# A ninth weight buffer, buffers in order of release, and the short expert's first gate and up moved into the long expert's first step

## What is computed

```python
def moe_swiglu(h, w_router, w_gate, w_up, w_down):
    logits = (t @ w_router)                       # 256 x 8
    top_vals, top_idx = lax.top_k(logits, TOP_K)  # 2 of 8
    top_w = jax.nn.softmax(top_vals, axis=-1)
    for e in range(N_EXPERTS):
        out = out + swiglu(t, w_gate[e], w_up[e], w_down[e]) * gates[:, e:e + 1]
return rms_norm(x, final_norm_g)
```

## Time and profile before

| | us |
|---|---|
| Median of 3 runs | 1364.99 (1363.95 to 1365.55) |
| The profiled execution | 1365.68 |
| Its span, first to last instruction | 1363.8 |
| PE busy | 1325.5 (97%) |
| VectorE busy | 787.8 (58%) |
| ScalarE busy | 658.2 (48%) |
| The queue of SP's transfers | 440.82 MB, 79.7% of 16 engines' span |
| Mean granted TensorE clock | 0.996 |

### The profile page before, as it was taken

How to read it: one execution, slowest core, us unless ns; L and a number is a source line. 1 busy time by engine, 2 the same in 40 slices (tenths; PEclk the granted TensorE clock), 3 DMA queues, 4 the chain that set the end, 5 groups by cost and what they waited for, 6 DMA issues and landing times.

```text
span 1363.8 us, 16923 instructions
## 1 busy us (share of the span) xinstructions
PE 1325.5 (97%) x6365; PEld 945.1 (69%) x6365; DVE 787.8 (58%) x912; ACT 658.2 (48%) x823; POOL 41.2 (3%) x45
## 2 busy tenths in 40 slices
PE   9999999999999999999999999999999999999996
PEld 8888788888888778765666656666555566665562
DVE  6555445555569668856466455565444565554463
ACT  5444344444454756544455454454444455544451
POOL 1000001000000010200000000000000000000000
PEclk9999999999999999999999999999999999999999
DMA  9745456555455518999999999999999999999995
GB/s 382 300 155 185 158 181 229 193 192 189 147 192 188 214 71 332 380 420 425 410 429 427 428 427 426 412 426 427 429 428 426 412 427 426 430 426 428 427 426 213
DMA packets 40448, 451.63 MB, mean 331 GB/s; under 512 B 4873, under 2 KB 5001, under 8 KB 8368
## 3 DMA queue, kind: packets, MB, share of 16 engines
q1 hardware_dynamic: 37408, 440.82, 79.7%
q0 software_dynamic: 2816, 9.63, 1.8%
q10 hardware_dynamic: 144, 0.09, 0.0%
HBM read 445.52 MB, written 6.55 MB: 331 GB/s over the span
## 4 chain that ended last, share of the span: by engine, by line
PE 78%; DMA 17%; DVE 2%; ACT 1%; issue 1%; POOL 0%; SPq 0%; DVEq 0%; ACTq 0%
PE psum L1968 19%; PE psum L1970 18%; PE psum L1969 18%; PE psum L2356 15%; DMA raw<-in_moe_w_gu 6%; DMA raw_more<-in_moe_w_gu 4%; DMA raw_first<-in_moe_w_gu 2%; DMA work<-in_moe_w_gu 2%; DMA raw<-in_moe_w_down 2%; PE psum L2014 1%; PE psum L2015 1%; PE psum L2016 1%; PE psum L2024 1%; DVE w_lo L1386 1%; ACT w_hi L1023 1%; PE psum L2394 1%
## 5 line engine op out<-in xcount | busy, mean ns | idle before, releaser
L1386 DVE TENSOR_TENSOR w_lo<-raw,w_hi 128x1024 fp32r<-128x1024 f32 (+1 forms) x150 | 265.7, 1782 | 224.2 <-ACT w_hi L1023 223.5
L1023 ACT CAST w_hi<-raw 128x1024 fp32r<-128x1024 f32 (+1 forms) x150 | 223.1, 1498 | 225.5 <-PE psum L1970 156.2
L1970 PE MATMUL psum<-w_hi,actA_lo 128*128 128x512 f32 (+1 forms) x752 | 291.2, 387 | 0.0
L1968 PE MATMUL psum<-w_hi,actA_hi 128*128 128x512 f32 (+1 forms) x644 | 257.1, 399 | 21.8 <-DVE w_lo L1386 20.6
L1969 PE MATMUL psum<-w_lo,actA_hi 128*128 128x512 f32 (+1 forms) x644 | 248.7, 386 | 0.0
L1968 PEld LDWEIGHTS psum<-w_hi,actA_hi 128*128 128x128 f32 x644 | 121.8, 189 | 66.3 <-DVE w_lo L1386 32.2
L1970 PEld LDWEIGHTS psum<-w_hi,actA_lo 128*128 128x128 f32 x752 | 141.9, 189 | 30.1
L1969 PEld LDWEIGHTS psum<-w_lo,actA_hi 128*128 128x128 f32 x644 | 122.2, 190 | 22.0
L2356 PE MATMUL psum<-raw,const 128*64 128x512 f32 x584 | 129.4, 595 | 0.1
L1968 PE MATMUL psum<-w_hi,actB_hi 128*128 128x512 f32 x292 | 114.8, 393 | 0.0
L1969 PE MATMUL psum<-w_lo,actB_hi 128*128 128x512 f32 x292 | 114.0, 390 | 0.0
(11 more groups left out here) (280 smaller groups left out, 1987.2 us busy)
## 6 DMA issues: line engine op xcount, KB each, us to landing
raw<-in_moe_w_gu SPq DMA_DIRECT2D x46, 2048.0 KB, 25.0
raw_more<-in_moe_w_gu SPq DMA_DIRECT2D x35, 2048.0 KB, 25.0
raw<-in_moe_w_down SPq DMA_DIRECT2D x23, 2048.0 KB, 26.4
raw_first<-in_moe_w_gu SPq DMA_DIRECT2D x17, 2048.0 KB, 25.6
raw_more<-in_moe_w_down SPq DMA_DIRECT2D x16, 2048.0 KB, 26.2
work<-in_moe_w_gu SPq DMA_DIRECT2D x14, 2048.0 KB, 27.0
raw<-in_ret_w_in SPq DMA_DIRECT2D x22, 1024.0 KB, 9.3
work<-in_moe_w_down SPq DMA_DIRECT2D x9, 2048.0 KB, 27.1
```

The lines of the kernel that those rows point to most:

```text
L1023: nc.scalar.copy(hi_of(u)[:, 0:size], raw_of(w, u)[:, 0:size]).then_inc(sem["hi_ready"], 1)
L1386: nc.vector.tensor_tensor(lo_of(u)[:, 0:size], raw_of(w, u)[:, 0:size], as_f32(hi_of(u)[:, 0:size]), ALU.subtract).then_inc(sem["lo_ready" ...
L1968: nc.tensor.matmul(dst, l_hi[:, k, cols], r_hi[:, kk, rcols], start=first, stop=False)
L1970: return nc.tensor.matmul(dst, l_lo[:, k, cols], r_hi[:, kk, rcols], start=False, stop=last)
```

## The change

- The buffers get a ninth one, number 8, over `work[0:4096]`, for blocks 13, 19 and 25 only. Block 13 waits until both gathers and the writing of the rows to DRAM are done.
- The buffers of blocks 5 to 48 come from a written table in place of the cycle. Blocks 5 and 6 go into buffers 7 and 0, and block 9 is issued behind them.
- The loop and the last pair use eight buffers for their first blocks (56 of 84 in a turn of the loop, 8 in the last pair) and seven for the rest.
- The final gain goes into buffer 4, and POOL loads it at the end, behind the read of y.
- TensorE's first steps: 4 parts of step 0; `short_gather`; a fifth part; the short gate and up; the last 3 parts; 4 parts of step 1; the turning of step 0; the other 4 parts; 4 down parts; the turning of step 1; the slot sums. Step 1's gate and up use other PSUM banks.
- ScalarE copies the short rows and the short gate and up in that place. VectorE ranks the places between the two halves of the long rows' residue and picks the short rows ahead of the third part's residue; its gate arithmetic, up to `rest_of_current(0)`, moves from behind the 20th part's residue to behind the ninth part's.

```diff
@@ work_order @@
         open_hidden("first", 0, G0, U0)
-        parts(8, ("first", "long_gate", 0), ("first", "long_up", 0))
-        open_hidden("first", 1, G1, U1)
+        parts(4)
+        o.open(("short_gather",), T1, ("short_rows", 1))
+        o.group(("short_gather",))
+        parts(1)
+        short_hidden("first", 0)
+        parts(3, ("first", "long_gate", 0), ("first", "long_up", 0))
+        open_hidden("first", 1, U1, T1)
         parts(4)
         long_turn("first", 0)
-        o.open(("short_gather",), T1, ("short_rows", 1))
-        o.group(("short_gather",))
...
         long_turn("first", 1)
-        short_hidden("first", 0)
@@ the tables @@
-        def ring_first(v):
-
-            return v if v < 5 else (0, 1, 5, 6, 7, 2, 3, 4)[(v - 5) % FIRST_RAW]
+        ring_first = [0, 1, 2, 3, 4, 7, 0, 5, 6, 1, 7, 0, 2, 8, 3, 4, 5, 6, 1, 8, 7, 0, 2, 3, 4, 8, 5, 6, 1, 7, 0, 2, 3, 4, 5,
+                      6, 2, 1, 7, 0, 3, 4, 1, 5, 6, 2, 7, 0, 3]
+        ring_more, ring_last = ring_first[-MORE_RAW:], ring_first[-EXPERT_RAW:]
+        ring_loop = ring_more * MORE_TURNS + ring_last * ((2 * ITEM_BLOCKS - MORE_TURNS * MORE_RAW) // EXPERT_RAW)
+        ring_end = ring_more + ring_last * (ITEM_BLOCKS // EXPERT_RAW)
...
-                + [work[:, 6400:6400 + 2 * UNIT]] + [more[:, :] for more in raw_more[0:2]])
-        final_gain = raw_more[1][:, 0:D]
+                + [work[:, 6400:6400 + 2 * UNIT]] + [more[:, :] for more in raw_more[0:2]]
+                + [work[:, 0:2 * UNIT]])
+        final_gain = twos[ring_more[0]][:, 0:D]
@@ SP @@
+                elif ring_first[v] == FIRST_RAW - 1:
+                    sp.wait_ge(sem["pe_done"], w.pe("short_gather"))
+                    sp.wait_ge(sem["rows_out"], 16 * TILES)
...
+            def user_before(v):
+
+                before = [u for u in range(v) if ring_first[u] == ring_first[v]]
+                if before:
+                    first_used(before[-1])
+                else:
+                    first_free(v)
...
-            first_free(FIRST_BLOCKS + 2)
-            load(FIRST_BLOCKS + 2, "down", None, 1, 0, False)
+            first_free(5)
             sp.wait_ge(sem["ranked"], 1)
             short_first = sp.value_load(expert_ids[0:1, 3 * EXPERT_PAIRS:3 * EXPERT_PAIRS + 1], min_val=0, max_val=N_EXPERTS - 1)
             for v in range(5, FIRST_BLOCKS):
-                long_split(n_dense + 4 * (v - 5) + 3)
+                if v > 5:
+                    user_before(v)
                 load(v, FIRST[v][0], short_first, *FIRST[v][2:], False)
+            user_before(FIRST_BLOCKS + 2)
+            load(FIRST_BLOCKS + 2, "down", None, 1, 0, False)
             load_pair(0)
@@ POOL @@
             move_rows(0)
-            pool.wait_ge(sem["pe_done"], w.pe("pair", "short_gu", STEPS - 1, 1))
-            load_gain(1)
...
+            pool.wait_ge(sem["pe_done"], w.pe("last", "short_gu", 2, 0))
             pool.wait_ge(sem["two_in"][w.ring(v)], w.block_in(v))
             pool.sem_inc(sem["back_asked"], 1)
             pool.dma_start(y_back.rearrange("p t k d -> p t (k d)"),
                            y_dram[P:, :].rearrange("(t p k) d -> p t (k d)", t=TILES, k=2)).then_inc(sem["y_in"], 16)
+            load_gain(1)
@@ ScalarE @@
+            hi_through(n_dense + 8)
+            short_rows(("short_gather",))
+            hi_through(n_dense + 9)
+            short_gu_out("first", 0)
             hi_through(n_dense + 11)
             long_silu("first", 0)
             hi_through(n_dense + 16)
             turned_hi("first", 0)
-            short_rows(("short_gather",))
             hi_through(n_dense + 19)
             long_silu("first", 1)
             hi_through(n_dense + 20)
             turned_hi("first", 1)
             hi_through(n_dense + 24)
-            short_gu_out("first", 0)
@@ TensorE @@
-                for half in range(2):
-                    pe.wait_ge(sem["long_lo"], half + 1)
-                    long_hidden("first", 0, units, range(4 * half, 4 * half + 4))
+                pe.wait_ge(sem["long_lo"], 1)
+                long_hidden("first", 0, units, range(4))
+                short_gather(("short_gather",))
+                pe.wait_ge(sem["long_lo"], 2)
+                long_hidden("first", 0, units, range(4, 5))
+                pe.wait_ge(sem["short_rows"], 1)
+                short_hidden("first", 0, 5)
+                long_hidden("first", 0, units, range(5, KC))
                 long_hidden("first", 1, units, range(4))
                 turn_hidden("first", 0)
-                short_gather(("short_gather",))
                 long_hidden("first", 1, units, range(4, KC))
                 long_down("first", 0, units, range(4))
                 turn_hidden("first", 1)
-                pe.wait_ge(sem["short_rows"], 1)
-                short_hidden("first", 0, 5)
                 slot_sums(("slots",), 0)
```

More of the change, by code:

```diff
@@ L617, in block_in, with place @@
             def block_in(self, v):
-                r = self.ring(v)
+                ring, i = self.place(v)
+                r = ring[i]
+                n = 16 * (ring[:i + 1].count(r) + (0 if ring is ring_first else first_loads[r]))
+                return n if self.turn is None else self.turn * (16 * loop_loads[r]) + n
+            def place(self, v):
                 if self.base == 0 and v < LOOP_BLOCK:
-                    return 16 * sum(self.ring(before) == r for before in range(v + 1))
-                n = first_loads[r] + 1 + (v - FIRST_BLOCKS) // EXPERT_RAW + (self.base - 1) * (ITEM_BLOCKS // EXPERT_RAW)
-                return 16 * n if self.turn is None else self.turn * (32 * ITEM_BLOCKS // EXPERT_RAW) + 16 * n
+                    return ring_first, v
+                if self.last:
+                    return ring_end, v - FIRST_BLOCKS
+                return ring_loop, v - FIRST_BLOCKS + (self.base - 1) * ITEM_BLOCKS
             def ring(self, v):
-                if self.base == 0 and v < LOOP_BLOCK:
-                    return ring_first(v)
-                return (2, 3, 4, 0, 1, 5, 6)[(v - FIRST_BLOCKS) % EXPERT_RAW]
+                ring, i = self.place(v)
+                return ring[i]
             def part_done(self, u):
@@ L896, in _ @@
                 load_pair(2)
-            w.turn, w.base, j = turns, 1, 0
+            w.turn, w.base, w.last, j = turns, 1, True, 0
             now, seen = experts_of(0), set()
@@ L989, in _ @@
                 move_rows(2)
-            w.turn, w.base = turns, 1
+            w.turn, w.base, w.last = turns, 1, True
             pool.wait_ge(sem["y_done"], w.at("y_done", 16 * 4))
             v = FIRST_BLOCKS + END_DOWN + 4
+            pool.wait_ge(sem["pe_done"], w.pe("last", "short_gu", 2, 0))
             pool.wait_ge(sem["two_in"][w.ring(v)], w.block_in(v))
@@ L1354, in _ @@
                 pair(2)
-            w.turn, w.base, w.units, split[0] = turns, 1, order.last_units, first_loop_unit + EXPERT_SPLIT
+            w.turn, w.base, w.units, w.last, split[0] = turns, 1, order.last_units, True, first_loop_unit + EXPERT_SPLIT
             for n in range(2, STEPS):
@@ L1800, in _ @@
             lo_through(n_dense + 2)
-            for g in range(2):
-                long_rows_rest(("gather",), g, 0)
+            long_rows_rest(("gather",), 0, 0)
+            in_rank_order(place_ranked, place)
+            long_rows_rest(("gather",), 1, 0)
             dve.sem_inc(sem["short_out"], 1)
-            lo_through(n_dense + 10)
-            in_rank_order(place_ranked, place)
+            lo_through(n_dense + 3)
             for t in range(TILES):
@@ L2513, in _ @@
                 pair(2)
-            w.turn, w.base, count[:] = turns, 1, loop_start
+            w.turn, w.base, w.last, count[:] = turns, 1, True, loop_start
             units = done + order.last_units
```

48 lines of the change are left out of this document (30 added, 18 removed).

## The result

| | before | after |
|---|---|---|
| Median of 22 runs each, us | 1364.82 (1362.93 to 1367.02) | 1366.93 (1363.3 to 1369.96) |
| Ratio, 95% interval | | 1.0015 (1.0009 to 1.0021) |
| The profiled execution, us | 1365.68 | 1366.78 |
| Its span, us | 1363.8 | 1365.0 |
| Mean granted TensorE clock | 0.996 | 0.993 |

The kernel became about 2 us slower (by the interval 1.2 to 2.9). The forecast was 1363.3 us with a range to 1366.2; the median lies outside it. By the 0.2% of the prediction (2.7 us) this is "no change", but 22 runs on each side tell even 0.15% apart from nothing. The two profiled executions differ by 1.1 us, and that is what can be followed in the trace.

The account below looks back on a forecast made before the run. The prediction took the start of the unbroken weight stream plus the bytes behind it as the bound. Anchor -0.45 and final gain -1.2 sum to -1.65 us, against the median of 1364.99 giving 1363.3 us, range 1360.5 to 1366.2.

Parts of the forecast that it names:

- What bounds the kernel: Whole kernel: the end is the time at which the weight stream starts to be unbroken, plus the bytes behind it.
- The new anchor: Start of the unbroken stream: block 19, issued behind block 13's last residue, lands at 597.95 + D; gain 2.35 - D, 0.45 us.
- D = +1.9: Ahead of the loop: its first step starts 1.9 us later than before, first product at 567.9.
- the cover is gone: Ahead of the loop: 7 us of short products no longer hide the last turning and copy before the first cast.
- upper bound of 2.3: Ahead of the loop: the most that the first step's delay D was allowed to be, 2.3 us.
- finds room: Kernel's end: the final gain's 512 KB, moved behind y, lands at 1349.7 in free DMA time; 1.2 us saved.
- slower rival: Kernel's end: the final gain lands at 1360.4, after its first use; +4.6 us, in all 1367.9 us; chance 0.06.
- near 545: Before the loop: the rows are written to DRAM near 545, so block 13's wait for them costs nothing.
- Blocks 5 and 6 early: Before the loop: blocks 5 and 6 land at 532.4 and 537.3, in time for the short products; effect nothing.
- the loop's eight buffers: In the loop: an eighth buffer gains nothing, since TensorE waits for bytes and the DMA engines are never idle.
- the rival of the late register reading: Before the loop: SP reads the expert's number late, block 5 is issued at 529.1; D 4.4, time 1365.8 us; chance 0.10.
- The rule of the Trainium skill that was weighed: In the loop: the added buffer would remove TensorE's 20.6 us of waits, giving 1344.4 us; as a rival, chance 0.03.

Follow-up runs that it names:

- late_block: casts_first with block 19's issue made to wait for the split of block 14's first part, 8.3 us later: 1369.48 us, ratio 1.0039 to the kernel before.
- filler: The changed kernel with eleven useless TensorE products in the pause ahead of the loop: 1364.91 us, ratio 0.9998 to the kernel before.
- rows_swap: casts_first with blocks 13 and 14 trading buffers (19, 23, 25 following), so block 13 skips the wait for the rows' writing: 1362.98 us, ratio 0.9984.
- release_order: casts_first with the buffer table rewritten so block 13 doesn't wait for the rows nor block 19 for block 13: 1361.36 us (0.9972), repeated 1361.07 us (0.9977).
- loop_only: The kernel before with only eight buffers for part of the loop and last pair, and the final gain behind y: 1364.92 us, ratio 0.9999.
- first_only: The changed kernel with seven buffers in the loop and the final gain loaded behind the first pair, as before: 1366.87 us, ratio 1.0013.
- casts_first: The changed kernel with the loop's first four casts and residues moved ahead of the copy of the last turned rows: 1362.52 us, ratio 0.9981.
- gain_early: casts_first with the final gain loaded ahead of the last blocks instead of behind the read of y: 1363.93 us, ratio 0.9991.

## Why the prediction was wrong

- **What bounds the kernel** (right). The start of the unbroken stream plus the bytes: a hole of 8.3 us in the stream, with no engine's work touched, costs 7.8 us at the end (late_block).
- **The new anchor is block 19 behind block 13's last residue** (right). Issue 0.16 us behind the residue, queue empty ahead of it.
- **D = +1.9, "the cover is gone"** (mechanism right, term mis-sized). The first product came at 568.02, forecast 567.9. But D was taken at that product, while block 13's residue is paced by what follows it. The step that failed is the one from the first product to block 13's last residue: I let the loop's first step run at its old pace behind the pause. At half the clock seven products took 1.5 us more, so D was 3.54, above my upper bound of 2.3. The anchor, forecast at a gain of 0.45, lost 1.2. filler keeps the wait and takes away only the slow products: D is 1.93, the anchor gains 0.4, and the loss is gone. The rows that would have priced them were in the trace of the kernel before: the longest wait of the earlier trace rows, 2.73 us, is followed by just these seven products in 3.13 us. I had not looked behind it.
- **The final gain "finds room" at the end** (wrong; the second term that failed). The 1.2 us left the stream, as the products at 1343.47 show against 1343.80 with an anchor that was 1.2 us later. They came back as a wait of 1.49 us for the last half block, 0.23 where the gain isn't loaded there. I had taken the DMA engines' 31% between 1345 and 1350 us as room, but the gain is issued at 1332.4, when the queue still holds the last blocks, and it lands with the last of them, after 19.5 us. The landing at 1349.7 was too early by 2.2 us (1332.41 + 19.5 = 1351.9); the danger was not the gain's own first use, as in my slower rival, but the block that it travels with. The 1.26 us by which it came later are about what the gain's own bytes take in the full stream, 1.2 us.
- **Rows out "near 545", block 13's wait nothing** (wrong number, no effect here). POOL asked at 541.34, but the later half landed 17.4 us after its issue in the full queue, which put block 13 at 559.60, and the rate fell to 238 GB/s from 560 to 562. Block 19's wait hid it: rows_swap takes the rows' wait away and changes nothing. Whether it counts once block 19's wait is gone is not shown by itself, since release_order takes both away.
- **Blocks 5 and 6 early, the loop's eight buffers: nothing** (right). Block 5 was issued at 522.88 us (forecast 524.4), and the short products came at 536.2 and 539.7 (forecast 535.9 and 539.4) without a wait, so the rival of the late register reading falls; loop_only is 0.9999. The rule of the Trainium skill that was weighed there ("Perfetto Trace Analysis", Identifying Performance Opportunities: repeated gaps can mean too little on-chip room for the next tile) would have allowed a time as low as 1344.4 us; no run comes near.

The sum: the forecast was -1.65; the anchor came out 1.65 worse (1.2 + 0.45) and the last half block 1.26 (1.49 - 0.23), which makes +1.3. The profiled executions differ by +1.1, the medians by +2.1; the 0.8 us between the terms and the medians are not accounted for by any trace. Of the range's bounds one was broken, the upper one on D, by 1.2 us; the final gain's term came out at its lower bound, nothing. Neither alone would have carried the forecast out of the range. Together they put the time at about 1366.2 us, the range's upper end.

## What to carry to other kernels

In a kernel bound by a full stream, find the one issue that starts it and cost every edit by what it does to that issue; what was won ahead of it (rows_swap) or by buffers behind it (loop_only) did not show in the time here. When a reordering takes the cover off a chain turning-copy-cast-product, move the casts of the next stage ahead of the copy in the same edit. A pause of TensorE can cost, beyond its own length, 1.5 us of products at half the clock behind it; look in the trace of before at what follows the longest waits. And 512 KB taken out of the middle of a full stream were not saved by putting them at its end: none of the four places tried was shown to be better than another.

## What the runs showed of the hardware

- A pause of 2.54 us was followed by a granted clock of 0.50, for seven 128x512 products, 1.5 us in all; ahead of the loop it showed in both profiles that had the pause (after and first_only) and in neither that didn't (casts_first, filler). The shorter pause of 0.89 us in the earlier trace rows had no slow product in its rows.
- The length of a wait alone doesn't decide it. Behind waits of 2.73 and 2.31 us (before) and 3.54 (late_block, at 883.78) about seven products were slow; behind 2.74 (release_order, at 1053.63) and 2.90 (gain_early, at 1270.44) none was, with a granted clock of 1.00. Behind the 1.91 us at 1058.13 in after four products started at full speed and seven after them 0.43 us apart. Behind the 1.76 us at 1210.42 in the kernel before none was slow.
- Two writes of 512 KB to DRAM landed 14.7 us (median of the two) after their issue among weight blocks, and 4.0 us in the kernel before, where the DMA engines were 69% busy from 554 to 556 us; a 512 KB load took 19.5, 11.1 or 8.2 us by its place at the end of the stream. A time to landing taken where the queue is in another state says little.
